# The recurrent stage of a hybrid decoder: U products issued in turn with the bars at a step's first hop and with the inner value products at its second, the inner products in bank 7

## The reference

```python
def step(state, inp):
    r_t, w_t, k_t, v_t, kk_t, a_t = inp
    sa = jnp.einsum('bhvk,bhk->bhv', state, -kk_t)
    state = (state * w_t[:, :, None, :]
             + sa[..., None] * (kk_t * a_t)[:, :, None, :]
             + v_t[..., None] * k_t[:, :, None, :])
    return state, jnp.einsum('bhvk,bhk->bhv', state, r_t)

_, y = lax.scan(step, s0, xs)
```

## Time and profile before

| what | us |
|---|---|
| median of 3 runs | 2978.84 |
| lowest and highest run | 2965.72 and 2980.3 |
| profiled execution, first to last instruction | 2974.8 |
| recurrent stage in it | about 350 to 790 |

### The profile page before, as it was taken

How to read it: one execution, slowest core, us unless ns; L and a number is a source line. 1 busy time by engine, 2 the same in 40 slices (tenths; PEclk the granted TensorE clock), 3 DMA queues, 4 the chain that set the end, 5 groups by cost and what they waited for, 6 DMA issues and landing times. The chain is left out here.

```text
span 2974.8 us, 56716 instructions
## 1 busy us (share of the span) xinstructions
PE 2791.2 (94%) x23069; PEld 2243.1 (75%) x23069; DVE 1870.3 (63%) x2527; ACT 1201.8 (40%) x2178; POOL 1305.4 (44%) x1112
## 2 busy tenths in 40 slices
PE   7999989999799999998999999988889999999998
PEld 5888777777667788887887777756667788887787
DVE  6333566666443756556986788867752865556895
ACT  3111343333233433334444766545542433334442
POOL 6344234444232545456554454422112555556653
PEclk9999899999799999999999999999999999999999
DMA  5333100010031233336543232342122233335651
GB/s 199 107 100 105 59 25 24 25 46 4 24 127 65 78 128 113 114 114 205 161 123 93 57 100 89 109 164 86 65 78 86 77 119 106 110 114 174 191 142 68
DMA packets 290602, 295.37 MB, mean 99 GB/s; under 512 B 11623, under 2 KB 223709, under 8 KB 289193
## 3 DMA queue, kind: packets, MB, share of 16 engines
q1 hardware_dynamic: 288440, 286.89, 30.6%
q10 hardware_dynamic: 1424, 4.83, 0.4%
q0 software_dynamic: 480, 0.03, 0.0%
HBM read 200.30 MB, written 88.65 MB: 97 GB/s over the span
## 5 line engine op out<-in xcount | busy, mean ns | idle before, releaser
L312 POOL TENSOR_TENSOR w_lo_b<-w_raw_b,w_hi_b 128x512 fp32r<-128x512 f32 (+3 forms) x540 | 748.0, 1388 | 672.8 <-ACT w_hi_b L346 669.5
L396 PE MATMUL ps<-b_hi,w_hi_b 128*128 128x512 f32 x1540 | 610.4, 396 | 9.2 <-issue 9.2
L396 PE MATMUL ps<-b_lo,w_hi_b 128*128 128x512 f32 x1540 | 602.7, 391 | 0.0
L396 PE MATMUL ps<-b_hi,w_lo_b 128*128 128x512 f32 x1540 | 602.3, 391 | 0.0
L346 ACT ACTIVATE w_hi_b<-w_raw_b 128x512 fp32r<-128x512 f32 (+3 forms) x498 | 295.2, 596 | 454.9 <-PE ps L3370 198.1
L396 PEld LDWEIGHTS ps<-b_hi,w_hi_b 128*128 128x128 f32 x1540 | 291.4, 189 | 74.7 <-issue 14.2
L396 PEld LDWEIGHTS ps<-b_lo,w_hi_b 128*128 128x128 f32 x1540 | 291.4, 189 | 63.9 <-issue 3.9
L396 PEld LDWEIGHTS ps<-b_hi,w_lo_b 128*128 128x128 f32 x1540 | 291.1, 189 | 61.1
L3370 PE MATMUL ps<-b_hi,w_hi_b 128*128 128x512 f32 x616 | 245.9, 399 | 24.3 <-DVE x_res L3187 23.8
L3370 PE MATMUL ps<-b_lo,w_hi_b 128*128 128x512 f32 x616 | 242.6, 394 | 0.0
L3370 PE MATMUL ps<-b_hi,w_lo_b 128*128 128x512 f32 x616 | 242.5, 394 | 0.0
(11 more groups left out here) (429 smaller groups left out, 5786.6 us busy)
## 6 DMA issues: line engine op xcount, KB each, us to landing
w_raw_b<-in_w_gate_up SPq DMA_DIRECT2D x88, 512.0 KB, 4.3
act_dram<-x_res SPq DMA_DIRECT2D x44, 512.0 KB, 6.1
sum_dram<-x_res SPq DMA_DIRECT2D x40, 512.0 KB, 2.9
w_raw_b<-in_w_down SPq DMA_DIRECT2D x28, 512.0 KB, 5.8
stage<-sum_dram SPq DMA_DIRECT2D x54, 256.0 KB, 3.8
stage<-act_dram SPq DMA_DIRECT2D x50, 256.0 KB, 4.2
w_raw_a<-in_a_w_in SPq DMA_DIRECT2D x23, 512.0 KB, 4.7
u_dram<-evac_a SPq DMA_DIRECT2D x16, 512.0 KB, 3.0
```

What stands on the lines that cost most here:

```text
L312: nc.gpsimd.tensor_tensor(self.wlo[:, r, 0:n, :], source, self.whi[:, r, 0:n, :].bitcast(F32), ALU.subtract).then_inc(self.w_lo, 1)
L396: mm = self.nc.tensor.matmul(self.ps[:, bank, :], w[:, r, k, :], h[:, block, k, :], start=(start and k == 0 and a == 0 and h is self.bh), ...
```

## The change

At a step's first hop the U products and the bars are issued block by block in turn (U, bars, U, bars, ...), behind the waits of both. The inner value products move from hop 1 to hop 2, where they are issued in turn with that hop's U, into bank 7 and no longer bank 2; their copy on ScalarE moves behind the `u_copy` of hop 2. Because bank 7 belongs to the side work, every hop's side work first waits for the inner copy (that of this step from hop 2 on), and the inner products wait for the last reader of bank 7. Piece 2, which writes banks 2 and 3, waits for `piece_dve` and not for the inner copy. No product is added or dropped.

```diff
@@ -1597,6 +1597,7 @@
             sums = ps[:, 6, 4 * C:4 * C + 16]
+            inner = ps[:, 7, 0:4 * C]
@@ -1755,6 +1756,7 @@
                 def side_work(s, l):
 
                     w, r = window(s), place(s, l)
+                    pe.wait_ge(mv_copied, min(s + 1 if l > 1 else s, S))
@@ -1794,7 +1796,7 @@
                         if i == 2:
                             pe.wait_ge(feat, p + 1)
-                            pe.wait_ge(mv_copied, n)
+                            pe.wait_ge(piece_dve, 6 * n)
@@ -1813,26 +1815,10 @@
-                    else:
-                        pe.wait_ge(piece_dve, 6 * n + 6)
-                        for t, b, h in blocks:
-                            u = 2 * t + h
-                            mm = mmul(ps[half[b], 2, cols64(0, u)], lak[half[b], u, :], tok[half[b], w3, u, TV, :], start=True, stop=True)
-                        mm.then_inc(mv_done, 1)
-
                 def tail(o, i):
...
-                    if i == "bars":
-                        pe.wait_ge(xx_added, xx_count[o, LEVELS])
-                        pe.wait_ge(mv_copied, o + 1)
-                        pe.wait_ge(y_added, o)
...
@@ -1865,17 +1851,70 @@
-                def inverse_u(n, l):
+                def u_waits(n, l):
                     pe.wait_ge(u_copied, u_count[n, l] - 1)
                     pe.wait_ge(join_done, join_count[n, l])
...
+                def bars_waits(o):
+                    pe.wait_ge(xx_added, xx_count[o, LEVELS])
+                    pe.wait_ge(mv_copied, o + 1)
+                    pe.wait_ge(y_added, o)
...
+                def inner_waits(n):
+                    pe.wait_ge(piece_dve, 6 * n + 6)
+                    w, r = window(n), place(n, 2)
+                    if r == 1 and w >= 3:
+                        pe.wait_ge(gn_scaled, 2 * (w - 3) + 2)
+                    elif r == 1:
+                        pe.wait_ge(g_act, 2)
+                    elif r == 6 and w == 1:
+                        pe.wait_ge(z_act, 2 * w + 1)
+                    elif r == 6 and w < PAIRS:
+                        pe.wait_ge(a_act, 2 * w + 2)
+                    elif r == 11 and w < PAIRS:
+                        pe.wait_ge(kk_used, 2 * w + 2)
+                    elif r == 16 and w < PAIRS:
+                        pe.wait_ge(bonus_done, 2 * w + 2)
+                    elif r == 16:
+                        pe.wait_ge(g_act, 2 * (w - 1) + 1)
+
+                def inner_block(n, t, b, h):
+                    u = 2 * t + h
+                    return mmul(inner[half[b], cols64(0, u)], lak[half[b], u, :], tok[half[b], n % 3, u, TV, :], start=True, stop=True)
+
+                def inverse_u(now, o, n):
+                    if now:
+                        u_waits(*now)
+                    if o is not None:
+                        bars_waits(o)
+                    if n is not None:
+                        inner_waits(n)
+                    for at in blocks:
+                        if now:
+                            u_last = u_block(*now, *at)
+                        if o is not None:
+                            bars_last = bars_block(o, *at)
+                        if n is not None:
+                            inner_last = inner_block(n, *at)
...
@@ -1903,11 +1942,9 @@
-                            inverse_u(*now_u)
-                        if l == 1 and s < S:
-                            piece(s, 5)
-                        if o >= 0 and l in (1, 2, 4):
-                            tail(o, {1: "bars", 2: "gh", 4: 1}[l])
+                        inverse_u(now_u, o if o >= 0 and l == 1 else None, s if l == 2 and s < S else None)
+                        if o >= 0 and l in (2, 4):
+                            tail(o, {2: "gh", 4: 1}[l])
                         side_work(s, l)
@@ -2022,7 +2059,7 @@
                     act.wait_ge(mv_done, n + 1)
-                    copy(tok[:, n % 3, :, MV, :], ps[:, 2, 0:4 * C].rearrange("p (u c) -> p u c", c=C)).then_inc(mv_copied, 1)
+                    copy(tok[:, n % 3, :, MV, :], inner.rearrange("p (u c) -> p u c", c=C)).then_inc(mv_copied, 1)
@@ -2048,7 +2085,7 @@
                             u_copy(s, l)
-                        if l == 1 and s < S:
+                        if l == 2 and s < S:
                             mv_copy(s)
```

More of the change, by code:

```diff
@@ L1815, in piece @@
                         mm.then_inc(piece_mm, 1)
-                    else:
-                        pe.wait_ge(piece_dve, 6 * n + 6)
-                        for t, b, h in blocks:
-                            u = 2 * t + h
-                            mm = mmul(ps[half[b], 2, cols64(0, u)], lak[half[b], u, :], tok[half[b], w3, u, TV, :], start=True, stop=True)
-                        mm.then_inc(mv_done, 1)
                 def tail(o, i):
                     p, q, w3 = o // STEPS, o % STEPS, o % 3
-                    if i == "bars":
-                        pe.wait_ge(xx_added, xx_count[o, LEVELS])
-                        pe.wait_ge(mv_copied, o + 1)
-                        pe.wait_ge(y_added, o)
-                        for t, b, h in blocks:
-                            u = 2 * t + h
-                            mm = mmul(ps[half[b], 4 + t, h * 2 * C:(h + 1) * 2 * C], xx[half[b], o % 3, 1, u, :],
-                                      tok[half[b], w3, u, MV:TA + 1, :].rearrange("p a c -> p (a c)"), start=True, stop=True)
-                        mm.then_inc(bars_done, 1)
-                    elif i == "gh":
+                    if i == "gh":
                         pe.wait_ge(bars_copied, o + 1)
@@ L1874, in inverse_u, with u_block @@
                         pe.wait_ge(xx_added, xx_count[n, l - 1])
-                    for t, b, h in blocks:
-                        u = 2 * t + h
-                        mm = mmul(ps[half[b], 6, cols64(0, u)], join[half[1 - b], l - 1, u, :], xx[half[1 - b], n % 3, 0, u, :], start=True, stop=True)
-                    mm.then_inc(u_done, 1)
+                def u_block(n, l, t, b, h):
+                    u = 2 * t + h
+                    return mmul(ps[half[b], 6, cols64(0, u)], join[half[1 - b], l - 1, u, :], xx[half[1 - b], n % 3, 0, u, :], start=True, stop=True)
@@ new lines, in bars_waits, with bars_block @@
+                def bars_waits(o):
+                    pe.wait_ge(xx_added, xx_count[o, LEVELS])
+                    pe.wait_ge(mv_copied, o + 1)
+                    pe.wait_ge(y_added, o)
+                def bars_block(o, t, b, h):
+                    u = 2 * t + h
+                    return mmul(ps[half[b], 4 + t, h * 2 * C:(h + 1) * 2 * C], xx[half[b], o % 3, 1, u, :],
+                                tok[half[b], o % 3, u, MV:TA + 1, :].rearrange("p a c -> p (a c)"), start=True, stop=True)
@@ new lines, in inner_block @@
+                def inner_block(n, t, b, h):
+                    u = 2 * t + h
+                    return mmul(inner[half[b], cols64(0, u)], lak[half[b], u, :], tok[half[b], n % 3, u, TV, :], start=True, stop=True)
[13 more added lines that the diff above has]
+                            inner_last = inner_block(n, *at)
+                    if now:
+                        u_last.then_inc(u_done, 1)
+                    if o is not None:
+                        bars_last.then_inc(bars_done, 1)
+                    if n is not None:
+                        inner_last.then_inc(mv_done, 1)
```

## The result

Beside each other on one chip, the kernel before took 2974.26 us (median of 20 runs, 2963.93 to 2984.46) and the changed one 2988.80 us (median of 20, 2970.50 to 3005.98). The ratio is 1.0046, 95% interval 1.0032 to 1.0060: the change costs some 14 us. The forecast was 2978.2, -0.6 us against the 2978.84 of the three runs before it. The time is inside the range of 2965 to 2992, but a loss of 14 us was not forecast.

What follows compares the result with a forecast made beforehand. TensorE's sequence was taken to set the recurrent stage's time. Hop 1's gain of 8.0 us less costs of 2.9, 3.7 and 0.8 gave -0.6 us on the 2978.84 median: 2978.2 us, range 2965 to 2992.

Steps and rivals of the forecast that it cites:

- The sum of the waits: Recurrent stage: all gains and costs from waits between engines together, -0.6 us, between -9 and +3.
- Hop 1, the wait for the add: U now waits for VectorE's y add: gains of 0.16 to 0.39 us in 17 steps, 0.78 in four; 8.0 us altogether.
- U finishes late: Hop 1: U's later end delays its copy, hop 2's XX and the group norm's square; costs 2.9 us, between 0 and 5.4.
- Hop 2: Inner in turn with U costs nothing itself; gh starting later loses 3.7 us, between 0 and 4.2.
- The seam: Hop 2: gh can no longer start while U's other quarters work; 0.17 us in each of 22 steps, 3.7 us.
- Steps 0 and 1: No gh covers the side work's new wait for the inner copy; costs 0.4 us each, 0.8 together.
- Other queues: GpSimd's join, SyncE's loads and VectorE's piece 4 lose nothing by the new order; costed at nothing.
- rival 4: TensorE's stalls for instructions move under the new wait or out of it; some 10 us either way, 5%.
- rival 3: New idle ahead of U in 17 steps lowers TensorE's clock; at most 8 to 25 us more, likelier 2987 us; 10%.
- rival 1: Hop 1: the y wait does not bite, 17 steps gain up to 0.5 us more; -9 us, 2970 us; 10%.
- rival 2: The two streams in turn do not run side by side, taking 1.29 and 0.94 us; 22 us more, 3000 us; 5%.
- the sign of the clock: Mark of a lower clock after the change: the stage's granted clock drops under 0.93.

Runs made afterwards that it cites:

- late_after: The changed kernel with the whole k, v and r loads started two pieces later; ratio to the kernel before 0.9991 (0.9974 to 1.0007).
- spread_after: The changed kernel with the 512 KB k, v and r loads cut into quarters of 128 KB; ratio to the kernel before 0.9993 (0.9981 to 1.0005).
- inner_alone: The changed kernel with the bars out of the turn again, behind U at hop 1; ratio to the kernel before 1.0040 (1.0019 to 1.0059).
- y_first: The changed kernel with VectorE's y add moved ahead of its piece 4; ratio to the kernel before 1.0036 (1.0015 to 1.0058).
- late_before: The kernel before with the whole k, v and r loads started two pieces later; ratio to the unedited kernel before 0.9986 (0.9968 to 1.0004).

## Why the prediction was wrong

**The sum of the waits held.** Take the stage's length, less half of its time at 1.2 GHz (my estimate of what that costs against 2.4), less the stalls. It is 393.3 and 391.5 us before, 393.3 and 390.9 after; with late loads 393.7 and 392.7; with cut loads 391.9 and 393.3 before, 393.3 after. (The estimate takes off a little too much: of two profiles of one kernel, the one with more time at 1.2 GHz comes out 2 us lower.) The three waits of steps 0, 1 and 23 that stand under "issue" add 1.9 to each of the changed ones. So the structure costs some 2 us, where -0.6 with bounds of -9 and +3 was the forecast. Its terms:

- *Hop 1, the wait for the add*: right. It stands in 17 cases, and U starts 0.14 us behind the add, not 0.06. U and bars in turn took 0.84 us, not 0.80. The two together leave of the gain of 0.16 to 0.39 in a step 0.03 to 0.16, and 0.30 in step 22 (from the y products of the step before to the last bars product, against before): 1.7 us in the 16 steps 3 to 22, and not 3.8 in 17. In steps 4, 8, 12 and 16 it is 0.75, forecast 0.78.
- *U finishes late*: too small. XX of hop 2 starts 0.75 us behind the bars' last product in the steps with the wait, where it was 0.45, and the U behind it keeps most of this: 0.26 to 0.33 us later in most steps, where 0.1 was forecast in seven and 0.2 in eleven. In steps 3 to 22 this is 3.6 to 3.9 us, and with steps 2 and 23 (0.3 and 0.77; in step 23 no piece 2 covers U's copy) some 5, where 2.9 was forecast between 0 and 5.4.
- *Hop 2*: U and inner in turn took 0.43 us in step 20, as said. The seam, 3.7 us in the sum, came to 0.02 a step: gh follows U's first start at 0.47 to 0.52 and not at 0.29, but its products then start within 0.35 to 0.38 us and not 0.56. This term was too large, and paid for the smaller gain and the later U. That the sum came out near was luck in part.
- *Steps 0 and 1*: 0.79 us of wait, by its place for the inner copy, in step 1, in the place that was named (the side work's new wait).
- *Other queues*: at nothing, and nothing showed.

**The step that failed** is the sentence "No product is added, so the stalls in which TensorE waits for instructions alone ("issue", 7.4 us at U) should stay, though their places may move." They rose from 16.7 and 19.0 us in the stage to 22.7 and 24.4. The step had two faults. First, I took the 7.4 us at U for a fixed cost and never asked what a stall is. In the traces nearly every one ends behind a 16 KB packet of queue 8. Some of these packets are due while loads hold the DMA engines. For the others it is argued, not shown, that TensorE gets through its 125 products faster than the packets follow each other: the shortest distance in any profile is 3.2 us, and one in twenty stretches of 128 products takes some 2.8 us or less before, 2.4 after, but the packets ahead of such stalls in the changed kernel came 3.7 to 7.1 us behind the one before. The change makes the dense parts denser by design and shifts each packet against the bursts. Stalls rose by 5 to 7 us in each of the three pairs of profiles (whole, late and cut loads), 1.9 of it the three ordinary waits. Second, rival 4 had the mechanism but not its sign and not what follows: "some 10 us either way", at 5%. It didn't come out symmetric: they rose in all three pairs.

**The clock** (rival 3) was priced for the wrong cause. Not the new idle of 0.3 to 0.5 us ahead of U brought it down: late_after keeps all of that idle, and its mean clock is 0.9736 (12 runs), that of spread_after 0.9734, the kernels before lie at 0.971 to 0.974. With the loads in their old place the changed kernel has 0.970 (20 runs) and 0.9693 (12), and so have inner_alone, in which that idle is gone (0.9682), and y_first (0.9690). Over the runs of one kernel, 0.001 of the mean clock goes with about 2 us. So the 0.002 between the two kernels' runs goes with some 4 us. That is an estimate: longer stalls and a lower clock come together in these runs, and two series of the kernel before differ by 0.002 as well.

**The account of the 14 us.** Stalls 5 to 6 (of it 2 the waits of steps 0, 1 and 23), the clock about 4, and 4 that I can't place: outside the stage the profiled executions differ by as much from one to the next. What is shown is that the whole, against the kernel before, goes when the loads are moved by two pieces. Not shown is how it divides, nor why the kernel before gains so much less by the same move: stalls in late_after are 7 us over those of late_before in the one profile of each (11.9 and 18.7), while their runs differ by 0.05%, give or take 0.25%. It may be that the clock, 0.9717 against 0.9736, happened to pay for the stalls there. So of a lasting part of 0 to 0.3% that these loads don't explain I can say only that spread_after shows it (10 us between the medians on one chip) and late_after leaves it open (4 us).

**The rivals**: rival 1 was wrong (the wait bites), rival 2 was wrong (0.84 and 0.43 us against 1.29 and 0.94). The rule of the Trainium skill (TensorE: Matmul & The Clock Gate, The mechanism) behind rival 2, that a weight load overlaps only with matmuls of another row group, did not decide here: blocks of U and inner read the same half and started 0.01 us apart. (The page excepts a load into the background weight buffer; no run shows whether it was one.) Of "what would show it", the signs of the structure appeared nearly as written (a wait of U for the add in 17 steps; 0.84 and 0.43 us), and the sign of the clock, a stage below 0.93, did not (0.95 and 0.98). They were looked for in one profiled execution, and this one ran 18 us below the median of its kind.

## What to carry to other kernels

Before packing an engine's instruction stream more tightly, look at what its "issue" gaps are: find the instruction queue's packets, the stalls that end behind them, and the large transfers that lie over them. Where such transfers are issued together, cutting them or moving them by two pieces was worth more here than the packing (some 15 us for the changed kernel; 4 to 11 for the kernel before, which is hardly clear of the noise), and it is best done first, since otherwise a good change can lose by where it happens to push a fetch. And judge a change by several runs and their clocks: here the profiled execution of the slower kernel was faster than that of the other.

## What the hardware showed that I had not expected

- TensorE's instructions come in packets of 16 KB on a queue of their own, one for every 125 products, and in the changed kernel a packet came 4.1 to 5.2 us after the start of three loads of 512 KB or of those near 650 us, with TensorE at a stand for 1.6 to 3.2 us. TensorE went on 1.2 to 1.6 us after a packet had landed, in nearly all stalls over 0.4 us of eighteen profiles.
- A wait whose count was reached long before cost some 0.05 us in this stream (289 of them 13 to 18 us; 72 of them 2 us, between -4 and 9).
- A TensorE stall of 2.9 us was followed by 6.8 us at 1.2 GHz, others of 1.6 to 3.5 us by 3 to 17 us or by none; the shorter stalls of the kernels with cut or moved loads were mostly followed by none.
- Products of two 64x64 streams in turn, one on each diagonal pair of quarters, started side by side, 32 records in 0.43 us, though blocks of both read the same half.
